# A causal mask moved from TensorE to VectorE in the second attention of a decoder trunk

## What is computed

```python
for i in range(S // 128):                     # four blocks of 128 queries
    q0, end = i * 128, (i + 1) * 128
    s = einsum('bhiqd,bhikd->bhiqk', q[:, :, :, q0:end], k[:, :, :, :end]) * 32 ** -0.5   # two maps a head
    mask = arange(end)[None, :] <= (q0 + arange(128))[:, None]
    p = softmax(where(mask, s, -inf))
    attn = p[:, :, 0] - lam * p[:, :, 1]
    outs.append(einsum('bhqk,bhkd->bhqd', attn, vh[:, :, :end]))
```

## Time and profile before

| what | us |
|---|---|
| runs of the kernel, median of 3 | 1808.89 |
| lowest and highest | 1799.23, 1811.03 |
| profiled execution, first to last instruction (the page gives this span, and no time beside it) | 1804.7 |
| TensorE products busy in it | 1592.4 |
| TensorE weight loads busy | 975.8 |
| VectorE busy | 583.3 |
| ScalarE busy | 285.9 |
| GpSimd busy | 159.0 |

### The profile page before, as it was taken

The page is one execution under the profiler, slowest core; times in us unless marked ns, Lnnn a source line. Parts: engine busy times, 40 slices in busy tenths (PEclk is TensorE's granted clock), DMA queues, the critical chain, the costliest instruction groups (busy, mean ns, idle before and its releaser), DMA issues.

```text
span 1804.7 us, 22281 instructions
## 1 busy us (share of the span) xinstructions
PE 1592.4 (88%) x9208; PEld 975.8 (54%) x9208; DVE 583.3 (32%) x1314; ACT 285.9 (16%) x694; POOL 159.0 (9%) x175
## 2 busy tenths in 40 slices
PE   7999989999799888787699999899997997988783
PEld 4445766557466455444344566664764664554441
DVE  2175336635121111221321842464432211112115
ACT  3131146320000000000123121651200000000001
POOL 0010000002211011110000100000031111111000
PEclk9999989998899999999999999999999999999997
DMA  9202012348999999999832120125589999999995
GB/s 323 88 32 88 1 47 86 123 199 352 423 424 423 424 424 423 423 423 419 360 127 93 49 62 5 43 94 232 201 361 424 423 423 424 425 422 424 423 419 204
DMA packets 72712, 486.58 MB, mean 270 GB/s; under 512 B 24413, under 2 KB 26397, under 8 KB 37792
## 3 DMA queue, kind: packets, MB, share of 16 engines
q1 hardware_dynamic: 62240, 468.81, 63.4%
q0 software_dynamic: 10368, 16.30, 2.5%
HBM read 472.24 MB, written 30.21 MB: 278 GB/s over the span
## 4 chain that ended last, share of the span: by engine, by line
PE 62%; DMA 25%; DVE 5%; issue 3%; SPq 3%; ACT 2%; POOL 1%; DVEq 0%; POOLq 0%; ACTq 0%
PE banks L623 12%; PE banks L962 12%; DMA RING<-in_w_gate 7%; PE banks L977 6%; PE banks L612 6%; DMA TOK<-in_w_up 6%; PE banks L915 5%; DMA RING<-in_w_down 3%; DMA TOK<-in_w_gate 2%; DMA SCAN<-in_w_up 2%; PE banks L940 2%; SPq L491 2%; PE banks L839 2%; PE banks L811 1%; PE banks L723 1%
## 5 line engine op out<-in xcount | busy, mean ns | idle before, releaser
L962 PE MATMUL banks<-RING,XS 128*64 128x256 f32 x2752 | 320.6, 389 | 48.9 <-DMA RING<-in_w_up 26.2
L962 PEld LDWEIGHTS banks<-RING,XS 128*64 128x64 f32 x2752 | 223.1, 140 | 157.7 <-issue 46.0
L623 PE MATMUL banks<-RING,XNT 128*128 128x512 f32 x512 | 225.2, 597 | 0.2 <-DMA RING<-in_w_in_blocks 0.2
L977 PE MATMUL banks<-RING,XS 128*64 128x512 f32 x768 | 176.7, 600 | 27.5 <-issue 14.1
L1789 DVE SCALAR_TENSOR_TENSOR XS<-banks,TABLE,XS 128x256 f32<-128x256 f32 x58 | 28.1, 484 | 435.6 <-PE banks L962 435.6
L623 PEld LDWEIGHTS banks<-RING,XNT 128*128 128x128 f32 x512 | 97.0, 192 | 118.3 <-issue 117.2
L1266 ACT ACTIVATE XS<-banks,TABLE 128x256 f32<-128x256 f32 x58 | 27.5, 474 | 798.0 <-PE banks L962 798.0
L977 PEld LDWEIGHTS banks<-RING,XS 128*64 128x64 f32 x768 | 60.8, 138 | 110.7 <-issue 110.7
L1831 DVE COPY XS<-banks 128x512 f32<-128x512 f32 x64 | 44.2, 691 | 216.5 <-PE banks L977 189.9
L2007 POOL DMA_INDIRECT y_rows<-XS,SOLVE x64 | 65.3, 1020 | 532.6 <-DVE XS L1831 510.3
L612 PE MATMUL banks<-XNT,RING 128*128 128x512 f32 x256 | 110.2, 592 | 0.0
(11 more groups left out here) (339 smaller groups left out, 1798.1 us busy)
## 6 DMA issues: line engine op xcount, KB each, us to landing
RING<-in_w_down SPq DMA_DIRECT2D x46, 2048.0 KB, 27.0
RING<-in_w_up SPq DMA_DIRECT2D x44, 2048.0 KB, 27.1
RING<-in_w_gate SPq DMA_DIRECT2D x42, 2048.0 KB, 26.2
RING<-in_w_in_blocks SPq DMA_DIRECT2D x12, 2048.0 KB, 9.6
TOK<-in_w_gate SPq DMA_DIRECT2D x12, 2048.0 KB, 32.4
TOK<-in_w_up SPq DMA_DIRECT2D x10, 2048.0 KB, 32.3
XNT<-in_w_down SPq DMA_DIRECT2D x8, 2048.0 KB, 30.9
TOK<-in_w_down SPq DMA_DIRECT2D x6, 2048.0 KB, 24.6
```

The costliest lines, as they stand in the source:

```text
L623: last = mm(bank[:, :], XNT[:, k, i * P:(i + 1) * P], w[:, k, :], start=(k == 0), stop=(k == KD - 1))
L962: last = mm(bank[f * CAP:(f + 1) * CAP, 0:256], rows[:, k, :], w[:, k, f * 256:(f + 1) * 256], start=(k == 0), stop=(k == KD - 1))
L977: last = mm(PS[5][n * CAP:(n + 1) * CAP, :], HT[:, j, f * CAP:(f + 1) * CAP], w[:, k, n * BN:(n + 1) * BN], start=(k == 0), stop=(k == KF ...
```

## The change

On TensorE the two mask products of each unit of the second attention are left out, and its score products end their sums themselves. On VectorE the loop over a unit's maps is replaced by one view over the unit's one or two banks: one wait for all its maps, one mask op over the last 128 columns of each, and one reduction that gives one or two maxima. For the first attention, with one map, the same ops as before come out.

```diff
--- before.py
+++ after.py
@@ -808,9 +808,7 @@
                                 for a in range(2):
                                     wait_bank(k0 + a)
                                     rows = slice((h % 2) * 64 + a * 32, (h % 2) * 64 + a * 32 + 32)
-                                    mm(score_bank(k0 + a)[:, 0:w], q[rows], kt[rows], start=True, stop=False)
-                                for a in range(2):
-                                    mm(score_bank(k0 + a)[:, i * P:w], cst("causal"), ident, start=False, stop=True, is_transpose=True).then_inc(scores, 1)
+                                    mm(score_bank(k0 + a)[:, 0:w], q[rows], kt[rows], start=True, stop=True).then_inc(scores, 1)
                             elif h % 2 == 0:
                                 for a in range(2):
                                     wait_bank(k0 + a)
@@ -1525,13 +1523,13 @@
                         if u < len(UNITS):
                             m, i, h = UNITS[u]
                             w = (i + 1) * P
-                            for a in range(MAPS[u]):
-                                k = FIRST_MAP[u] + a
-                                bank = PS[SCORE_BANKS[k % 4]]
-                                dve.wait_ge(*at(layer, scores, k + 1))
-                                if m == "A":
-                                    link(V.scalar_tensor_tensor(bank[:, i * P:w], later, NEG, bank[:, i * P:w], ALU.mult, ALU.add))
-                                V.tensor_reduce(nmx[:, k:k + 1], bank[:, 0:w], AX.X, ALU.max, negate=True).then_inc(maxed, 1)
+                            k, n = FIRST_MAP[u], MAPS[u]
+                            lo = SCORE_BANKS[k % 4] * BN
+                            banks = PSALL[:, lo:lo + n * BN].rearrange("p (a t) -> p a t", a=n)
+                            dve.wait_ge(*at(layer, scores, k + n))
+                            own = banks[:, :, i * P:w]
+                            link(V.scalar_tensor_tensor(own, later[:, None, :].to_broadcast([P, n, P]), NEG, own, ALU.mult, ALU.add))
+                            V.tensor_reduce(nmx[:, k:k + n], banks[:, :, 0:w], AX.X, ALU.max, negate=True).then_inc(maxed, n)
                         if 1 <= u <= len(UNITS):
                             n = u - 1
                             m, i, h = UNITS[n]
```

## The result

The changed kernel takes 1838.34 us (median of four runs, 1830.77 to 1847.24); the kernel before, measured beside it, 1806.88 (1799.23 to 1811.03). The ratio is 1.0194, 95% interval 1.0160 to 1.0227: slower by 31 us, and outside the range of the prediction.

A forecast was written before the change was run, and what follows sets the result against it. TensorE was taken to bound the attention stage, with small waits for the softmax. Unit shifts and savings gave +0.95 us a layer: 1804.7 + 4.2 + 1.9 = 1810.8 us, with 1799 to 1820 for 8 in 10.

The forecast's parts named there:

- The sizes of the operations: Second attention, per unit: TensorE saves 0.22 us (0.21 taken), mask op 0.42, merged reduction 1.22 to 0.42; VectorE 12 us busier.
- The hand-over from the mask op to the reduction: On VectorE, the step between the mask op and the reduction behind it, put at 0.03 us.
- The waits: TensorE waiting for softmax results: unit 4 from 1.28 to about 2.0 us, unit 10 from 0.18 to 1.1; unit 27 +0.72.
- Units 22 to 24: VectorE runs without a break through the other mixer's end and TensorE follows; +0.12 us for the three together.
- The sum: Shifts and savings of a layer's second-attention units added up: +0.95 us a layer, +1.9 us for both.
- A DMA share of 0.00: Reading that the DMA share is 0.00 in the attention stage, roughly 238 to 342 us and 1130 to 1232 us.
- what lies around the span: Time outside the profiled span of 1804.7 us, taken as 4.2 us from the median run of 1808.89.
- A stretch more at the lower clock: Rival: longer waits drop the second layer's clock as in the first behind unit 4; +6.6 us, 1817.4 us; chance 0.20.
- TensorE as the only bound: Rival: every mask turn taken out counts in the attention stage; -6.7 us, 1802.2 us; chance 0.15.
- Exps late everywhere: Rival: later exps land on TensorE in all units through ScalarE's order of work; +16.8 us, 1825.7 us; chance 0.08.
- unit 19: Model for seven free units: output copy ends a microsecond before TensorE's product, so no wait; 7 x -0.21 = -1.47 us.

The follow-up runs named there:

- first fill: Changed kernel with identity turns nobody reads in TensorE's waits: 18 in step 5, 10 in step 11, 10 ahead of the third turned output; 1804.19 us, ratio 0.9992.
- The two filled kernels of the table: Kernel before with its own waits filled, 1797.40 us; changed kernel with 6 and 8 more fill turns in steps 23 and 24, 1802.07 us.
- step 5 filled: Changed kernel with only 18 identity turns in step 5, where TensorE waits behind unit 4; 1822.96 us, ratio 1.0098.
- the last table: Filled kernels against the kernel before (1804.17 us): before 1797.40, after 1802.07, wide mask op with one reduction for each map 1797.74 us.
- unit 10 made late: Kernel before with two unneeded reductions on VectorE ahead of unit 10's first maximum, once a layer; 1828.06 us, ratio 1.0110.
- two maxima: Changed kernel with the wide mask op kept but one reduction for each map again; 1815.66 us, ratio 1.0058.
- map by map: Changed kernel with a separate mask op and reduction for each map, TensorE's mask turns still out; 1819.57 us, ratio 1.0085.

## Why the prediction was wrong

**The sizes of the operations** held: taking out a unit's mask turns shortens TensorE's work by 0.22 us, as forecast (unit 4, from its first score product to the end of the turn behind: 1.60 us before, 1.38 after); the wide mask op 427 ns (0.42 forecast), the reductions 1225 down to 425 ns (1.22 to 0.42), VectorE 11.5 us busier (12). The hand-over from the mask op to the reduction is 0.10 us rather than 0.03 (247.95 + 0.43 to 248.48), too little to matter.

**The waits** held nearly: unit 4 from 1.28 to 2.34 us (about 2.0 forecast), unit 10 from 0.18 to 1.24 (1.1), unit 27 from 0.21 to 1.34 in the first layer (+1.13; +0.72 forecast). Of unit 4's 1.06 us more, 0.23 is TensorE being done earlier: counted from the first score product its output product comes 0.83 us later, for +0.73 in the sum. Units 22 to 24, +0.12 in the sum, come out near it too: a wait of 0.80 us is new there, but the work around it (300.04 to 314.28 before, 310.33 to 324.81 after) is only 0.24 us longer.

**The sum** of +1.9 us is borne out to a few microseconds, for the case that the clock is the same on both sides: with 34 us at half clock in both, the profile of the changed kernel with its first fill is 3.0 us longer than that of the kernel before. The two filled kernels of the table differ by 1802.07 - 1797.40 = +4.7 us in their medians, with 30 turns a layer more in the second. Two readings beside the sum were wrong and don't move it. A DMA share of 0.00 is that of two windows only (0.54 from 300 to 320 us before). And what lies around the span is some 1.8 us (1847.24 and 1845.4 after), not 4.2; the sum goes by the median run all the same.

**The step that failed** is the rival "A stretch more at the lower clock": its chance of 0.20 and its size, one stretch of 6.6 us. I priced the waits of units 4, 10 and 27 at their own length and let the clock be a matter of one more stretch in the second layer behind unit 4. Units 4 and 10 brought one each in both layers, four where there had been one, and the lower-clock time at the ends of the stages grew from 14 to 58 us in the profiled run as well. At unit 10 I saw no clock risk at all, since its wait had cost no stretch before; at 1.24 us it has one in each layer. My price for a stretch was fair (6.6 us, against 0.41 x 20 = 8.2 by the stages), my count was not. What I gave as the argument against, that "the second layer runs the same steps with the same waits and kept its clock there", spoke of a wait of 1.28 us that kept the clock in one layer and lost it in the other: the row said that this place could go either way, and the change lengthened its wait.

The Trainium skill, "TensorE: Matmul & The Clock Gate", section "HAM oscillation", which I had set beside one layer of two, says that waits between bursts of products bring the array to half rate. The changed kernel agrees in both layers; the wait of 1.24 us at 1172.68 with step 5 filled, which kept its clock, shows that not every wait does it here. The Trainium skill, "TensorE: Matmul & The Clock Gate", section "PE-mode transpose", says that turns don't count as work for the clock as products do. The filled runs show that turns do hold it: with nothing but 18 of them in the wait at unit 4 the clock stayed at 1.00, where the changed kernel fell to 0.50.

**The other rivals:** TensorE as the only bound (1802.2 us) fell with the last table. Exps late everywhere (1825.7) has the right side for the wrong reason: unit 19 has no wait here either.

**What stays open:** the falls at the ends of the stages, whose place and length shift from run to run and do not go with one wait; what tips a wait of 1.24 or 1.28 us one way or the other (it isn't the layer: the kernel before loses the clock at unit 4 in the first, and with unit 10 made late in the second), and why four runs of the changed kernel spread over 16 us. The mean clock goes with the time (0.960 in the run of 1830.77 us, 0.945 in that of 1847.24).

## What to carry to other kernels

Where TensorE is the bound and the granted clock dips in a stage, price a longer wait of TensorE not by its length but by what may follow it: here a microsecond more of waiting was in most cases followed by a stretch that cost 6 to 8 us. Before moving work onto the engine whose result TensorE waits for, look at each wait that the move lengthens, and give the first consumer its input early rather than merge two small operations into a larger one. Where a wait can't be shortened, turns that nobody reads can be placed in the wait itself: here they held the clock, and the same turns elsewhere brought nothing back.

## What the runs showed that I had not expected

- A wait of one to two microseconds in these attention stages can go with some 20 us at 1.2 GHz. At units 4 and 10 each of the 14 waits of 1.63 to 2.46 us in these profiles had 17 us or more at half clock. Waits of 1.24 and 1.28 us went either way: 1.24 lost the clock in both layers of the kernel after and kept it in the second layer with step 5 filled, 1.28 lost it in one layer of two. Behind 0.18 us (before), 0.38 (filled), 0.64 (two maxima) and 0.72 (map by map) no such stretch stands. The length doesn't decide alone: the kernel before waits 1.24 us at another line of the stage, and the clock holds until 1211.

```profile
1152.72 0.66 PE L829 MATMUL banks<-CF,XNT 128*128 128x128 f32 x4 [1.24 <-DVE XNT L1547]
```

- 76 turns of 0.12 us (18 take 2.19 us), 9 us of added work on the engine that bounds the stage, took the ratio from 1.0194 to 0.9992.
- Taking the mask turns off TensorE showed as nothing, with the clock lost (ratio 1.0194 without them, 1.0181 with them) as with the waits filled (0.9960 and 0.9962).
